# Even experts with eight weight tiles of their own, a reordered beginning and a smaller descriptor scratch, in a decoder-layer kernel

## The reference

```
x = x + head_group_mixer(rms_norm(x, g_mix))     # w_in 1024x2048, two convolutions, a scan, w_out 1024x1024
x = x + cross_attention(rms_norm(x, g_xa), ...)  # w_q, w_k, w_v, w_o 1024x1024; 8 cached keys and values
x = x + routed_experts(rms_norm(x, g_moe))       # top 4 of 32 experts:
#   gu = xb @ w_e1[e] + b_e1[e]     w_e1[e] is 1024 x 2048, 8 MB
#   h  = (clip(u) + 1) * swish(min(g, 7))
#   rows = h @ w_e2[e] + b_e2[e]    w_e2[e] is 1024 x 1024, 4 MB
y = rms_norm(x, g_final)
```

## Time and profile before

| | us |
|---|---|
| median of 3 runs | 1238.9 (1238.03 to 1239.23) |
| the profiled execution, its own time | 1240.22 |
| its span, first to last instruction | 1238.6 |
| TensorE busy | 1159.6 (94%) |
| weight loads of TensorE busy | 564.2 (46%) |
| VectorE busy | 331.3 (27%) |
| ScalarE busy | 200.7 (16%) |
| GpSimd busy | 45.3 (4%) |
| moved by DMA | 457.43 MB (10^6 bytes), mean 369 GB/s |
| mean granted TensorE clock | 0.979 |

### The profile page before, as it was taken

One profiled execution on the slowest core, in us unless ns is written; L12 is line 12 of the kernel. 1 busy time (PEld: TensorE's weight loads), 2 busy tenths in 40 slices (PEclk: granted clock), 3 DMA queues, 4 the chain that ended last, 5 costly groups with the idle time before them and its releaser, 6 DMA issues.

```text
span 1238.6 us, 14414 instructions
## 1 busy us (share of the span) xinstructions
PE 1159.6 (94%) x5536; PEld 564.2 (46%) x5536; DVE 331.3 (27%) x801; ACT 200.7 (16%) x448; POOL 45.3 (4%) x87
## 2 busy tenths in 40 slices
PE   8999999899999999999999899989898989999996
PEld 6887888587343343333333333323232323233332
DVE  3795523515212212021212121120202121212113
ACT  3114212303010110111010111101011101010102
POOL 4100001100000000000000000000000000000000
PEclk9999999897999999999999999999999999999999
DMA  9389333994999999999999999999999999999993
GB/s 300 102 276 300 119 123 120 325 422 175 387 426 428 427 428 429 426 428 428 428 427 429 426 428 427 429 427 428 427 427 428 428 428 428 428 428 427 428 426 150
DMA packets 65608, 457.43 MB, mean 369 GB/s; under 512 B 5523, under 2 KB 34411, under 8 KB 40869
## 3 DMA queue, kind: packets, MB, share of 16 engines
q1 hardware_dynamic: 62576, 452.00, 89.0%
q10 hardware_dynamic: 1117, 3.04, 0.7%
q0 software_dynamic: 1888, 2.02, 0.6%
HBM read 453.71 MB, written 3.81 MB: 369 GB/s over the span
## 4 chain that ended last, share of the span: by engine, by line
PE 48%; DMA 46%; DVE 4%; ACT 1%; issue 1%; ACTq 0%; SPq 0%; POOL 0%; DVEq 0%
DMA ring<-in_w_e 45%; PE ps L1641 18%; PE ps L1337 11%; PE ps L1660 6%; PE ps L1356 3%; DVE ring L1017 2%; PE ps L1616 1%; PE ps L1607 1%; PE ps L1522 1%; PE ps L1560 1%; PE ps L1284 1%; PE ps L1273 1%; PE ps L1650 1%; PE ps L1471 0%; PE ps L1278 0%
## 5 line engine op out<-in xcount | busy, mean ns | idle before, releaser
L1641 PE MATMUL ps<-ring,mixed 128*64 128x512 f32 x1536 | 346.2, 596 | 37.1 <-DMA ring<-in_w_e 37.1
L1660 PE MATMUL ps<-ring,mixed 128*64 128x512 f32 x1024 | 235.3, 614 | 0.7 <-issue 0.7
L1641 PEld LDWEIGHTS ps<-ring,mixed 128*64 128x64 f32 x1536 | 104.9, 137 | 262.7 <-issue 182.5
L1178 DVE TENSOR_SCALAR mixed<-ps 128x512 f32<-128x512 f32 x32 | 22.1, 692 | 579.9 <-PE ps L1641 579.9
L1660 PEld LDWEIGHTS ps<-ring,mixed 128*64 128x64 f32 x1024 | 73.1, 140 | 160.0 <-issue 147.0
L740 ACT ACTIVATE mixed<-mixed 128x512 f32<-128x512 f32 x32 | 20.2, 630 | 513.6 <-DVE mixed L1178 513.6
L1616 PEld LDWEIGHTS ps<-mixed 128*128 128x128 f32 x512 | 62.2, 199 | 25.2 <-issue 25.2
L750 ACT ACTIVATE mixed<-ps 64x512 f32<-64x512 f32 x64 | 37.9, 592 | 217.5 <-PE ps L1660 217.2
L1616 PE MATMUL ps<-mixed 128*128 128x128 f32 x512 | 68.1, 289 | 0.8 <-DVE mixed L1108 0.8
L1641 PE MATMUL ps<-mixed 128*64 128x512 f32 x256 | 58.0, 595 | 6.7 <-DMA mixed<-in_w_e 6.7
L1165 DVE SCALAR_TENSOR_TENSOR mixed<-mixed,gates 128x1024 f32<-128x1024 f32 x15 | 19.3, 1285 | 160.0 <-ACT mixed L750 160.0
(11 more groups left out here) (304 smaller groups left out, 793.4 us busy)
## 6 DMA issues: line engine op xcount, KB each, us to landing
ring<-in_w_e SPq DMA_DIRECT2D x160, 2048.0 KB, 23.3
low<-in_w_e SPq DMA_DIRECT2D x15, 2048.0 KB, 27.5
mixed<-in_w_e SPq DMA_DIRECT2D x15, 2048.0 KB, 31.9
ring<-in_w_in SPq DMA_DIRECT2D x8, 1024.0 KB, 15.7
ring<-in_cache_mem_k SPq DMA_DIRECT2D x8, 1024.0 KB, 4.8
ring<-in_cache_mem_v SPq DMA_DIRECT2D x8, 1024.0 KB, 8.5
ring<-in_w_k SPq DMA_DIRECT2D x4, 1024.0 KB, 8.9
ring<-in_w_v SPq DMA_DIRECT2D x4, 1024.0 KB, 12.5
```

The source lines that it names most:

```text
L1178: dve.tensor_scalar(g1, ps[0][:, :], LIMIT, None, ALU.min).then_inc(S["g_clamped"], 1)
L1641: m = pe.matmul(ps[gu][CAP * i:CAP * i + CAP, :], xeT[:, k, CAP * e2:CAP * e2 + CAP], w[:, D * gu + 512 * i:D * gu + 512 * i + 512], start ...
L1660: m = pe.matmul(ps[3][CAP * i:CAP * i + CAP, :], hTv[:, k % 4, CAP * (k // 4):CAP * (k // 4) + CAP], ring[:, s, D * (k % 2) + 512 * i:D * ...
```

## The change

To free them, `acc` moves into `xnt`, `hh` shares `g1`'s place, `be2` and a one-row `gfin_row` move into `tok` and are fetched earlier by ScalarE, and GpSimd spreads the final gain over the partitions near the end.
2. **Tiles.** An even expert takes all its eight up tiles from `low`, `high`, `fourth`, `fifth`, `spare` (`even_up`), an odd expert all from ring slots 0 to 7. Both use ring slots 8 to 11 for the down weights.
3. **Fills.** `spare` is filled for expert 0 during the attention's keys, `fourth` and `fifth` before the expert stage begins. A pair has 13 fills (five for an even expert's up weights, of 2, 2, 1, 1, 2 MB) where it had 12. `EARLY_PAIRS` is 6.
4. **The beginning.** The 8 samples' transposes go together into a bank of their own; ScalarE makes `xn` straight from PSUM; the squares are summed by ScalarE along the token-major rows (`accum_out`), put on a diagonal by VectorE, and spread by three matmuls with ones. Tile 1 of the projection comes ahead of that. Seven small parameter DMAs move from ScalarE's list to GpSimd's, and `mem` behind the second `w_in` tile in SP's.

The diff, cut to its core:

```diff
-EARLY_PAIRS = 4
+EARLY_PAIRS = 6
+SINGLES = (4, 5)
...
+        fourth = mixed[:, MIXW + 2 * LC * P + KD * TOK - 3 * SLOT:MIXW + 2 * LC * P + KD * TOK - 2 * SLOT]
+        spare = sb("spare", [P, 2 * SLOT])
...
+        fifth = xnf[:, 0:SLOT]
-        head = [v[:, SLOT * i:SLOT * i + SLOT] for v in (low, high) for i in range(2)]
+        even_up = [v[:, SLOT * i:SLOT * i + SLOT] for v in (low, high) for i in range(2)] + [
+            fourth, fifth] + [spare[:, SLOT * i:SLOT * i + SLOT] for i in range(2)]
...
+                    if kind == "kc" and i == 2:
+                        sp.dma_start(spare[:, :], first_weight(0, 6)).then_inc(S["spare_filled"], 16)
...
-            for s in range(HEAD_SLOTS, W_SLOTS, 2):
-                fill(0, s, freed_after(MOE0 + s + 1 - RING))
-            for s in range(0, HEAD_SLOTS, 2):
+            for s in range(0, W_SLOTS, 2):
                 fill(1, s, freed_after(MOE0 + s + 1 - RING))
+            fill(0, 8, freed_after(MOE0 + 9 - RING))
+            refill(0, 4, freed_after(MOE0 + W_SLOTS - 1 - RING))
+            fill(0, 10, freed_after(MOE0 + 11 - RING))
...
+            sp.wait_ge(S["logit_done"], 1)
+            refill(0, 5, freed_after(MOE0 + 11 - RING))
+            EVEN_FILLS = (0, 2) + SINGLES + (6,)
+            for s in sorted(EVEN_FILLS, key=lambda s: FIRST_ORDER.index(s)):
+                refill(2, s, used(0, FIRST_ORDER.index(last_of(s))))
+            down_half(1, 1)
...
             with sp.Fori(1, EARLY_PAIRS) as q:
-                odd_half(q)
-                rest(2 * q, 2 * q)
-                even_half(q + 1)
-                rest(2 * q + 1, 2 * q + 1)
+                odd_up(q)
+                down_half(2 * q, 2 * q)
+                even_up_half(q + 1)
+                down_half(2 * q + 1, 2 * q + 1)
             with sp.Fori(EARLY_PAIRS, PAIRS - 1) as q:
-                rest(2 * q, 2 * q)
-                odd_half(q)
-                rest(2 * q + 1, 2 * q + 1)
-                even_half(q + 1)
+                down_half(2 * q, 2 * q)
+                odd_up(q)
+                down_half(2 * q + 1, 2 * q + 1)
+                even_up_half(q + 1)
...
             for k in range(KD):
-                act.wait_ge(S["x_copied"], k + 1)
-                act.activation(xn[:, k, :], xT[:, k, :], ACT.Copy, scale=par[:, C_GMIX + k:C_GMIX + k + 1]).then_inc(S["xn_ready"], 1)
-                act.activation(sq[:, k, :], xT[:, k, :], ACT.Square).then_inc(S["x_squared"], 1)
+                act.wait_ge(S["x_turned"], k // 2 + 1 + k // 4)
+                act.activation(xn[:, k, 0:SEQ], ps[IN_BANK[k // 2]][:, SEQ * (k % 2):SEQ * (k % 2) + SEQ], ACT.Copy,
+                               scale=par[:, C_GMIX + k:C_GMIX + k + 1]).then_inc(S["xn_ready"], 1)
+            for t, (t0, rows) in enumerate(TT):
+                act.activation(squares[t][0:rows, :], x0[0:rows, t, :], ACT.Square,
+                               accum_out=xss[0:rows, t:t + 1]).then_inc(S["x_squared"], 1)
...
-    nc = bacc.Bacc("TRN2", target_bir_lowering=False, num_devices=1)
+    nc = bacc.Bacc("TRN2", target_bir_lowering=False, num_devices=1, dynamic_dma_scratch_size=2048)
```

More of the change, by code:

```diff
@@ L169, in build @@
         assert pos[0] == MIXER_W
+        squares = [v.rearrange("p c t -> p (c t)")[:, 0:D] for v in (zg, gc, xc)]
+        diag = th.rearrange("p c t -> p (c t)")[:, 0:3 * P].rearrange("p (t m) -> p t m", t=3)
         stage_a = av.rearrange("p c t -> p (c t)")[:, 0:P]
@@ L195, in build @@
         gT = part(2 * P)
-        g1, u1, tg, hh, hT = (part(512) for _ in range(5))
+        g1, u1, tg, hT = (part(512) for _ in range(4))
+        hh = g1
         hTv = hT.rearrange("p (j s) -> p j s", j=4)
@@ L397, in _, with last_of @@
[L397 to L401, removed]
+            sp.wait_ge(S["logit_done"], 1)
+            refill(0, 5, freed_after(MOE0 + 11 - RING))
+            EVEN_FILLS = (0, 2) + SINGLES + (6,)
+            def last_of(s):
+                return s if s in SINGLES else s + 1
+            for s in sorted(EVEN_FILLS, key=lambda s: FIRST_ORDER.index(s)):
+                refill(2, s, used(0, FIRST_ORDER.index(last_of(s))))
@@ L516, in _ @@
                 bias(e)
+            pool.wait_ge(S["be2_loaded"], 32)
+            pool.wait_ge(S["freed"], RING * (NE - 2) + freed_after(MOE0 + 5))
+            pool.partition_broadcast(gfin, gfin_row, P).then_inc(S["gfin_ready"], 1)
             pool.wait_ge(S["nblk_ready"], 1)
@@ L631, in _ @@
                 act.dma_start(dst, src).then_inc(S["rows_stored"], 16)
+            act.dma_start(be2, a["b_e2"][0]).then_inc(S["be2_loaded"], 16)
+            act.dma_start(gfin_row, a["g_final"]).then_inc(S["be2_loaded"], 16)
             act.wait_ge(S["rows_stored"], 16 * 6)
@@ L1269, in _ @@
                     pe.wait_ge(S["xb_loaded"], 16)
-                if k >= 4:
-                    pe.wait_ge(S["x_copied"], k - 3)
-                for t, (t0, rows) in enumerate(TT):
-                    m = pe.transpose(ps[IN_BANK[k % 4]][:, t0:t0 + rows], x0[0:rows, t, k * P:(k + 1) * P], ident[0:rows, 0:rows])
-                m.then_inc(S["x_turned"], 1)
-            pe.wait_ge(filled[START["in"] % RING], 16 * fills_before(START["in"]))
-            for k in range(KD):
-                pe.wait_ge(S["xn_ready"], k + 1)
-                m = pe.matmul(ps[0][:, 0:TOK], wslot(START["in"])[:, k, 0:P], xn[:, k, :], start=(k == 0), stop=(k == KD - 1))
@@ L1279, in _ @@
-            m.then_inc(S["in_done"], 1)
-            def norm_sum(n):
-                for k in range(KD):
-                    pe.wait_ge(S["x_squared"], KD * n + k + 1)
+                for t in range(2):
+                    m = pe.transpose(ps[IN_BANK[k // 2]][:, SEQ * (k % 2) + P * t:SEQ * (k % 2) + P * t + P],
+                                     x0[:, t, k * P:(k + 1) * P], ident[:, :])
+                if k % 2:
+                    m.then_inc(S["x_turned"], 1)
+            pe.wait_ge(filled[START["in"] % RING], 16 * fills_before(START["in"]))
@@ new lines, in _ @@
+            pe.wait_ge(S["x_copied"], 3)
+            for o in range(2):
+                if o == 1:
+                    pe.wait_ge(S["x_copied"], 6)
+                for k in range(KD):
+                    pe.wait_ge(S["xn_ready"], k + 1)
+                    m = pe.matmul(ps[o][:, 0:TOK], wslot(START["in"])[:, k, P * o:P * o + P], xn[:, k, :],
+                                  start=(k == 0), stop=(k == KD - 1))
+                m.then_inc(S[("in_done", "freed")[o]], 1)
+            pe.wait_ge(S["consts"], 2)
@@ L1284, in norm_sum @@
+            for t, (t0, rows) in enumerate(TT):
+                pe.wait_ge(S["x_copied"], 7 + t)
+                m = pe.matmul(ps[5][:, t0:t0 + rows], ones[0:rows, :], diag[0:rows, t, 0:rows], start=True, stop=True)
+            m.then_inc(S["sum_done"], 1)
+            def norm_sum():
+                for k in range(KD):
+                    pe.wait_ge(S["x_squared"], 3 + k + 1)
                     m = pe.matmul(ps[5][:, 0:TOK], ones[:, :], sq[:, k, :], start=(k == 0), stop=(k == KD - 1))
                 m.then_inc(S["sum_done"], 1)
-            pe.wait_ge(S["consts"], 2)
@@ L1604, in rounds @@
                     if q is None:
-                        m = pe.matmul(ps[bank + i][0:rows, :], gateT[:, t0:t0 + rows], be2[0:NE, cols], start=True, stop=True)
+                        m = pe.matmul(ps[bank + i][0:rows, :], gateT[:, t0:t0 + rows], be2[:, cols], start=True, stop=True)
                     else:
```

159 lines of the change are left out of this document (92 added, 67 removed).

## The result

| | before | after |
|---|---|---|
| median, us | 1238.86 (1238.03 to 1239.23, 4 runs) | 1228.85 (1228.13 to 1230.1, 4 runs) |
| ratio to before, 95% interval | | 0.9919 [0.9907, 0.9932] |
| profiled execution, its own time, us | 1240.22 | 1228.78 |
| its span, us | 1238.6 | 1227.1 |
| GpSimd busy, us | 45.3 | 50.8 |

The kernel is faster by 10.0 us by the medians and by 11.4 by the two profiled executions; 13.9 was forecast. The time lies inside the range, 3.9 us above the predicted one.

The account below looks back on a forecast made before the run. The full weight-DMA pipe of the expert stage was taken as the bound, TensorE before it. Tiles 9.8 - hole 1.4 + beginning 5.5 = 13.9 us gained, for a median of 1225.0 us, range 1220 to 1232 (forecast's own 1221 to 1229).

Parts of the forecast that it names:

- The bound: Expert stage: a full DMA pipe; the end is its filling time plus 2.45 us per MB left plus a fixed tail.
- The four tiles: Before the pipe is full, 4 MB more of expert weights are fetched in idle DMA time: 9.8 us gained.
- The hole: At the change of loops, the fill of down(12) waits until TensorE has used down(11): 1.4 us lost, once.
- The beginning: From TensorE's first transpose to tile 4 on `sq`: ends at 26.6 instead of 32.17 us, 5.5 us gained.
- The two tiles: At the beginning, behind the first weight's landing at 11.2 us: 7.1 us for two projection tiles.
- the low end of its range: The beginning gains only 2 us, since two tiles at half the clock would cost up to 3.5 us.
- The basis: The 13.9 us were taken off the runs' median, 1238.9 us, for the prediction, not off the profiled execution's 1240.2.
- The added fills: Expert stage: 13 fills a pair instead of 12, 15 more in all, taken to cost nothing in the full pipe.
- Rival 3: Each of 15 added fills shows its fixed 2.8 us in the pipe: 42 us more, 1267 us; chance 0.03.
- Rivals 1, 2 and 4: Large hole, TensorE late: 1232.6 us (0.08); beginning gains nothing: 1230.5 (0.11); four tiles gain nothing: 1233.4 (0.04).
- the signs of being right: `sq` tiles at 26 to 27 us, 2 MB moved early, landings 14 us earlier at 29.4 us spacing, hole 1 to 3.
- what was to show the forecast wrong: Last landings' spacing grows, DMA rate drops below 425 GB/s, or the first expert's up product starts after 302 us.

Follow-up runs that it names:

- e4: The changed kernel with 4 MB of expert 1's up tiles fetched only after TensorE has begun expert 0: 1236.76 us, ratio 0.9983.
- e1: The changed kernel with the old beginning (old transposes, old sum of squares, small parameters on ScalarE's list): 1234.45 us, ratio 0.9959.
- e7: The changed kernel with three fills of each pair cut into two halves of 1 MB, same bytes and order: 1235.25 us, ratio 0.9968.
- e2: The kernel before with the new beginning alone (transposes, `xn`, squares, order of small DMAs): 1235.36 us, ratio 0.9969.
- e8: The kernel of e3 plus nine matmuls of constants, result unread, while TensorE waits for the prompt: 1225.34 us, ratio 0.9889.
- e6: The kernel before with the 2 KB descriptor scratch alone: 1238.95 us, ratio 0.9998.
- e3: The changed kernel with the change of loops spread over two pairs, up tiles standing between any two down fills: 1227.31 us, ratio 0.9901.

## Why the prediction was right, and where its sizes were off

**The bound was right.** The expert stage is a full pipe before and after, the tail is fixed, and the end moves by what the filling of the pipe and the bytes left then give. The sizes missed to one side: hole and beginning together made the kernel some 3.5 us slower than forecast, and the time is inside the range because the range was wide (the forecast's own was 1221 to 1229).

**The four tiles: 9.8 us, right.** e4 gives 7.9 for taking them back, and its rows account for the other 1.9.

**The hole: 1.4 us forecast, 3.2 measured, 4.9 in e1.** The mechanism was right (the fill of down(12) waits for down(11), with nothing else queued), and TensorE was not late, as forecast: it stood waiting. What was mis-sized is the delay of a fill. I took 2.8 us over the moving time from a lone fill and counted one such delay, where the wait has two: one until TensorE knows that the first half has landed, and one until the next fill flows. The stretches at the hole in fine steps, and the chain, show what happens:

```profile
620.00:631.00 11.00, 10.01 (x60) 4.64 (x58) 2.67 (x4) 3.57 (x11) 0.56 (x1) 1.00 1.00 427
631.00:632.00 1.00, 1.00 (x8) 0.36 (x6) 0.00 (x0) 0.00 (x0) 0.00 (x0) 1.00 0.61 252
632.00:633.00 1.00, 0.81 (x4) 0.00 (x0) 0.00 (x0) 0.00 (x0) 0.00 (x0) 1.00 0.28 117
633.00:634.00 1.00, 0.00 (x0) 0.00 (x0) 0.00 (x0) 0.00 (x0) 0.00 (x0) 1.00 0.30 66
634.00:635.00 1.00, 0.96 (x6) 0.40 (x8) 0.00 (x0) 0.00 (x0) 0.00 (x0) 1.00 1.10 197
635.00:636.00 1.00, 1.00 (x8) 0.38 (x6) 0.00 (x0) 0.00 (x0) 0.00 (x0) 1.00 0.72 246
```

```profile
608.52 25.47 DMA ring<-in_w_e
634.04 3.65 PE ps L1722 x16
```

SP's list just then:

```profile
632.99 0.33 SPq L374 DMA_DIRECT2D ring<-in_w_e  x1
```

The stream runs dry at about 631.6 us, but TensorE gets the second half only at 634.04, some 2.4 us after its data. The first half is late by the same delay: its data ended about 4.9 us before 631.6, at 626.7, and TensorE began on it at 629.16. Its 3.65 us there end at 632.81, and SP issues the next fill at 632.99, by then 1.4 us into the hole, as forecast. What the sum left out comes after: the stream is back at its rate only from 636 us on, and the three microseconds from 633 to 636 (66, 197 and 246 GB/s) lose (3 x 428 - 509) / 428 = 1.8 us more. The Trainium skill, DMA: Bandwidth & Descriptors (Anatomy of one DMA) says of the DMAs that GpSimd issues that most of their fixed 2 us is the confirmation that the last byte has landed. The 2.4 us here, for DMAs that SP issues, are of that size. Behind a full queue such a delay costs little bandwidth (e7); it costs all of it once the next issue depends on it.

**The beginning: 5.5 us forecast, 3.8 by e2's median.** The weight's landing was right (10.90 against 11.2 us). The two tiles were mis-sized: 7.97 us from the first to the sum (10.90 to 18.87) instead of 7.1, since TensorE came to them from idling and ran them at less than its rate; e8 shows the same tiles at 7.22 us. The forecast had this only in the low end of its range, since the granted clock in the first 12 us was 1.00. It is 1.00 there in all traces, and still the two tiles take 8.13 to 9.22 us in the six that share this beginning; the change's own trace is the fastest of the six. Three short matmuls cost 0.9 instead of 0.6. The first tile on `sq` is thus 4.6 us earlier, 4.0 from e6 (32.02) to e2 (28.02). That gain arrives at the experts: TensorE begins expert 0's down product 4.5 us earlier in e2 than in e6 (324.70 there):

```profile
320.18 8.71 PE ps L1699 x32
```

At the first refill only 2.8 us are left (328.33 to 325.50), because this product took 8.71 us in e2, at a granted clock of 0.66 from 320 to 325 us, and 7.02 in e6. So e2's rival, that the gain hangs on where the clock falls, holds for some 1.7 us of it in these two traces.

**The basis: the median, rightly.** No term of the sum came from a place where the executions differ. The difference of two traces would have misled: the 5.27 us between before and the change at the first refill look like the forecast 5.5 and are not. The change leads by 4.56 us at the first tile on `sq`, by 3.1 at 80 us, by 5.8 at 250 us (the 9.39 us of L1522 in before are in this) and by 4.9 at the down product, as the granted clock falls at other places in either trace.

**The added fills: nought forecast, between nothing and 2 us.** Rival 3 fell: e7's price of an added fill is 0.08 to 0.12 us, not 2.8. One of the reasons given against it does not count: the two 1 MB fills of `low` were issued at 243.34 and 246.27 us and landed some 11.6 us later, for the most part ahead of the stretch from 255 to 280 us.

**The sum by medians.** 9.8 for the tiles, less 3.2 for the hole, plus 3.8 for the beginning, is 10.4; measured are 10.0. The remaining 0.4 would be 0.03 us for each of fifteen added fills, within what the medians can tell. Rivals 1, 2 and 4 fell too: TensorE is early at the hole, the beginning gained, and e4 shows the tiles' worth. Of the signs of being right, the 2 MB moved early and the unchanged spacing came; the `sq` tiles (27.61 us for 26 to 27), the landings (11.6 us earlier for 14) and the hole (3.2 us for 1 to 3) missed by the sizes above. Of what was to show the forecast wrong, one thing came by half: the rate over the long stretch is 425 GB/s instead of 428, the edge I had named, and the hole alone makes 428 x 3.2 / 860 = 1.6 of the 3 (e3, without it, has 427 from 345 to 1190 us, the change 425).

**Open.** Why the granted clock falls where it does. It falls in every trace between 60 and 75, between 225 and 260 and between 285 and 310 us, at other microseconds in each, and in all but e6 between 315 and 330 us. Idle time alone does not tell it: in the change it is 1.00 up to 60 us and 0.56 from 60 to 62, with TensorE busy for 1.51 of the two microseconds from 56 and for 1.93 of the two from 58. Also open are 0.7 us of the longer hole of e1 and 0.7 of the hole's 3.2 that e3 does not get back. None of this was tried further.

## What to carry to other kernels

In a full stream of weights, count the bytes that are on chip when the stream becomes the bound; each MB there is worth its moving time once, and where it is fetched hardly matters so long as it is idle time. When the order of fills is changed midway, look for a fill that overwrites what the fill just before it brought: it empties the queue for a landing and a use, and other fills between the two (e3) take that away. Before a gain is read off two traces, compare pieces of the chain that the change does not touch (here a product that took 7.02 us or 8.71), or a fall of the clock in one execution is counted as a gain or a loss.

## What the runs showed of the hardware

- The record of the granted clock does not tell all: 1.00 in the first 12 us, while eight transposes took 1.97 us, and 1.13 when TensorE had been kept busy since 2.89 us. The two tiles at 10.9 us took 8.13 to 9.22 us in six traces at a record of 1.00, and 7.39 with TensorE kept busy.
- The same product of 32 matmuls took 7.02 us at a granted clock of 1.00 and 8.71 where 0.66 was granted over five microseconds. Two kernels with the same TensorE instructions, before and e6, differ in this.
- An added DMA of 1 MB in a full queue cost 0.08 to 0.12 us of the stream, a small part of the 2.4 us that a 2 MB one took from the end of its data to TensorE's start. Where the queue had run dry, 1.8 us more were lost from the next issue to the full rate.
- GpSimd's DMAs of this kernel lost nothing by a descriptor scratch of 2 KB.
